# PEER neuron table on one core: 32 of the 384 dense tokens move to the gathered side, and the gathers are placed anew

## The reference, cut to what matters

```python
q = (t @ w_query).reshape(T, PEER_HEADS, 2, PEER_HALF)
s = jnp.einsum('thpk,pnk->thpn', q, sub_keys)
s_val, s_idx = lax.top_k(s, PEER_TOPK)                 # 16 of 128 keys, twice per head
cand = s_val[..., 0, :, None] + s_val[..., 1, None, :]
best, pos = lax.top_k(cand.reshape(...), PEER_TOPK)    # 16 experts per head
expert = ...                                           # 8 heads x 16 = 128 experts per token
gate = jax.nn.softmax(best, -1)
act = gelu(einsum('td,ted->te', t, u_emb[expert])) * gate
out = einsum('te,ted->td', act, v_emb[expert])
```

## Time and profile before

| | |
|---|---|
| median of the three runs | 3464.65 us |
| the profiled execution | 3466.85 us |
| its span | 3465.0 us, 1.85 us lie around it |
| granted TensorE clock, mean | 0.992 |
| TensorE matmul busy | 98% of the span |
| VectorE, ScalarE, GpSimd busy | 62%, 34%, 53% |
| moved by DMA | 874.71 MB, 252 GB/s over the span |

### The profile page before, as it was taken

The page is one execution under the profiler, slowest core; times in us unless marked ns, Lnnn a source line. Parts: engine busy times, 40 slices in busy tenths (PEclk is TensorE's granted clock), DMA queues, the critical chain, the costliest instruction groups (busy, mean ns, idle before and its releaser), DMA issues.

```text
span 3465.0 us, 44031 instructions
## 1 busy us (share of the span) xinstructions
PE 3378.7 (98%) x16931; PEld 2932.8 (85%) x16931; DVE 2155.6 (62%) x3280; ACT 1186.4 (34%) x1632; POOL 1829.8 (53%) x904
## 2 busy tenths in 40 slices
PE   6999999999999999999999999999999999999998
PEld 3688888766888899999999999998887888888887
DVE  2288887746414759993766676644655566556656
ACT  3322221234223232223555556533232232222223
POOL 1210000213444355676666666666877777777775
PEclk8999999999999999999999999999999999999999
DMA  9655643565423236776677777788888878878872
GB/s 380 245 191 202 217 163 115 176 229 204 172 97 146 86 141 234 265 295 267 265 302 300 311 270 284 313 314 332 339 309 317 335 290 342 332 281 313 340 278 108
DMA packets 184618, 874.71 MB, mean 252 GB/s; under 512 B 16621, under 2 KB 77501, under 8 KB 97844
## 3 DMA queue, kind: packets, MB, share of 16 engines
q1 hardware_dynamic: 122160, 525.38, 41.1%
q0 software_dynamic: 38688, 281.15, 20.4%
q10 hardware_dynamic: 23652, 66.69, 5.1%
HBM read 803.78 MB, written 69.32 MB: 252 GB/s over the span
## 4 chain that ended last, share of the span: by engine, by line
PE 85%; DVE 7%; DMA 3%; POOL 2%; issue 1%; ACT 1%; ACTq 0%; SPq 0%; DVEq 0%; POOLq 0%
PE bank L2120 80%; PE bank L2381 2%; DMA ring<-in_w_mod 2%; PE bank L2498 1%; POOL split L807 1%; DMA ring<-in_v_emb 1%; PE bank L2355 1%; DVE b L1880 1%; POOL low L765 1%; DVE rows_a L1819 1%; PE bank L2128 1%; DVE b L1860 0%; DVE rows_c L1819 0%; PE bank L2481 0%; DVE tiny L1875 0%
## 5 line engine op out<-in xcount | busy, mean ns | idle before, releaser
L807 POOL TENSOR_TENSOR split<-ring,split 128x1024 fp32r<-128x1024 f32 x544 | 1343.2, 2481 | 569.4 <-ACT split L1145 567.2
L2120 PE MATMUL bank<-h_hi,split 128*128 128x384 f32 (+1 forms) x4608 | 1221.8, 341 | 8.2 <-POOL split L807 6.9
L2120 PE MATMUL bank<-split,a_split 128*128 128x512 f32 x4608 | 1051.4, 390 | 15.2 <-POOL split L807 15.0
L1145 ACT ACTIVATE split<-ring 128x1024 fp32r<-128x1024 f32 x544 | 574.0, 1060 | 1437.2 <-PE bank L2120 1257.9
L2120 PEld LDWEIGHTS bank<-split,a_split 128*128 128x128 f32 x4608 | 864.5, 188 | 201.8 <-POOL split L807 18.5
L2120 PEld LDWEIGHTS bank<-h_hi,split 128*128 128x128 f32 x4608 | 839.7, 188 | 29.6 <-POOL split L807 8.8
L2120 PE MATMUL bank<-h_lo,split 128*128 128x384 f32 (+1 forms) x2304 | 785.6, 341 | 0.0
L2120 PEld LDWEIGHTS bank<-h_lo,split 128*128 128x128 f32 x2304 | 433.5, 188 | 9.5
L1995 DVE TENSOR_TENSOR acc<-acc,bank 128x512 f32<-128x512 f32 x180 | 121.9, 682 | 331.0 <-PE bank L2120 331.0
L2120 PE MATMUL bank<-hT_hi,w_hi 128*128 128x512 f32 (+1 forms) x768 | 289.3, 377 | 5.3 <-POOL ring_lo L727 2.2
L2120 PE MATMUL bank<-hT_lo,w_hi 128*128 128x512 f32 (+1 forms) x768 | 287.2, 374 | 0.0
(11 more groups left out here) (318 smaller groups left out, 3846.0 us busy)
## 6 DMA issues: line engine op xcount, KB each, us to landing
ring<-in_u_emb SPq DMA_DIRECT2D x128, 1024.0 KB, 4.8
ring<-in_v_emb SPq DMA_DIRECT2D x128, 1024.0 KB, 10.4
ring<-in_w_mod SPq DMA_DIRECT2D x48, 1024.0 KB, 8.2
ring<-in_w_in SPq DMA_DIRECT2D x44, 1024.0 KB, 5.9
ring<-in_w_mod SPq DMA_DIRECT2D x64, 512.0 KB, 4.7
neurons<-tiny ACTq DMA_DIRECT2D x128, 192.0 KB
gate_table<-b ACTq DMA_DIRECT2D x6, 4096.0 KB, 15.0
weigh<-neurons SPq DMA_DIRECT2D x32, 768.0 KB
```

Source lines behind the costliest of these rows:

```text
L807: nc.gpsimd.tensor_tensor(split[:, r % 2, 1, at].bitcast(F32R), ring[:, r % 4, :, :].rearrange("p k n -> p (k n)")[:, at], split[:, r % 2, ...
L1145: nc.scalar.activation(split[:, q % 2, 0, at].bitcast(F32R), ring[:, q, :, :].rearrange("p k n -> p (k n)")[:, at], ACT.Copy)\
L2120: last = mm(out_, left[a].bitcast(F32R), right[b].bitcast(F32R), start=start and n == 0, stop=stop and n == 2)
```

## The change

The last 32 tokens of the third dense tile (EXTRA = 32) are taken out of the neuron matmuls, which have TN = 352 columns instead of 384. Their 32 x 128 slots are spread over four groups of partitions: partition 32g + t holds slot 32g + m of token t in gather m, so that 32 more gathers of `u_emb` and 32 more of `v_emb`, each of 128 rows, carry them. One more plain DMA brings the 32 tokens' rows, copied four times over the partitions, in place of the last tile's rows before their dots; ScalarE copies it into `bank_rows` (neuron unit 119). The v sums of the four groups are copied to SBUF, and four matmuls with a selection matrix (`sel`, not rounded) add them over the groups into the last tile's banks in sweep units 41, 43, 45 and 47. The search, the table and the sweep's matmuls still take all 384 tokens; the neurons of the 32 are zero.

`h2_hi` and `h2_lo` are laid out in blocks of 32 tokens, where it was 128, in the query projection too. ScalarE's and TensorE's loops over the sweep are unrolled in part. The order of the gathers comes from a list: `ROW_UNIT[n]` is the unit in which VectorE uses n. Worked out for the 321 rows (0 to 127 are the u rows of the last tile, 128 the plain one, 129 to 160 the 32 u rows more, 161 to 192 the 32 v rows, 193 to 320 the 128 v rows):

- one a unit in units 3 to 115, two in units 48, 56, ... 112, two a unit in 116 to 125, four in 126;
- in the sweep, two a unit in units 0 to 6 and one in unit 8: the last of the dots;
- v rows from sweep unit 11 to unit 116, at most two a unit, none where k = 7: 160 in 93 units (it was 128 from unit 3 to 115);
- a u row is gathered behind r = 16 + unit - 1, as before, a v row behind r = 16 + unit (with unit counted on from 128), one unit later in relation to its use than before.

```diff
+EXTRA = 32
+EG = P // EXTRA
+TN = TD - EXTRA
+U_ROWS = SLOTS + 1 + EXTRA
+ALL_ROWS = U_ROWS + EXTRA + SLOTS
...
+def row_units():
+
+    at = list(range(3, 3 + PRE - 3))
+    for unit in range(PRE, NK - 2):
+        twice = unit >= PRE + CHUNKS * CHUNK_UNITS or (EXTRA > 16 and unit % 8 == 0)
+        at += [unit] * (2 if twice else 1)
+    at = at[:U_ROWS - 4] + [NK - 2] * 4 if len(at) > U_ROWS - 4 else at + [NK - 2] * 4
+    unit = NK
+    while len(at) < U_ROWS:
+        if unit % 8 != 7:
+            at += [unit] * min(2, U_ROWS - len(at))
+        unit += 1
...
-            h2_hi = region("h2_hi", 8192, search)[:, :].rearrange("p (j k t) -> p k j t", j=LT, t=P)
+            h2_hi = region("h2_hi", 8192, search)[:, :].rearrange("p (g k t) -> p k g t", k=KT, t=EXTRA)
...
+                if n == SLOTS:
+                    pool.wait_ge(e_moved, 16 * 3 * EG)
                 if n >= 3:
                     pool.wait_ge(rows_used, n - 2)
...
+                if n == SLOTS:
+                    pool.dma_start(gathered_rows[n % 3], extra_dram[:, :]).then_inc(gathered[n % 3], 16)
+                    return
...
-                if 0 <= r - (U0 + 2) < SLOTS:
-                    gather_rows(r - (U0 + 2))
-                for m in range(SLOTS):
-                    if V0 + 2 + m - m // 8 == r:
-                        gather_rows(SLOTS + m)
+                for n in range(ALL_ROWS):
+                    if U0 + ROW_UNIT[n] - (n < U_ROWS) == r:
+                        gather_rows(n)
...
+                if r == 4:
+                    act.wait_ge(h2_made, 2)
+                    for g in range(EG):
+                        act.dma_start(extra_dram[g * EXTRA:(g + 1) * EXTRA, :], sh2_row[extra, :]).then_inc(e_moved, 16)
...
-                nc.scalar.activation(neuron_out[:, q % 2, :], bank[:, 4 + q % 2, 0:TD], ACT.Gelu)\
+                nc.scalar.activation(neuron_out[:, q % 2, 0:TN], bank[:, 4 + q % 2, 0:TN], ACT.Gelu)\
...
+                if k == ROW_UNIT[SLOTS]:
+                    rows = gathered_rows[SLOTS % 3]
+                    act.wait_ge(gathered[SLOTS % 3], 16 * (SLOTS // 3 + 1))
+                    act.wait_ge(rows_used, SLOTS)
+                    nc.scalar.activation(bank_rows[:, 0:D - P], rows[:, 0:D - P], ACT.Copy)
+                    nc.scalar.activation(h2_last, rows[:, D - P:D], ACT.Copy).then_inc(rows_used, 1)
...
+                if unit == E_COPY:
+                    act.wait_ge(rows_used, U_ROWS + EXTRA)
+                    nc.scalar.activation(sum_e, bank_rows, ACT.Copy).then_inc(e_copied, 1)
...
+                if k == 8:
+                    nc.vector.scalar_tensor_tensor(sc2_row[wide, :], x2[wide, JD - 1, :], rstd2[wide, JD - 1:JD],
+                                                   sc2_row[wide, :], ALU.mult, ALU.mult).then_inc(a2_made, 1)
...
             weigh_group(0)
-            dot(NK - 5)
+            dot(ROW_UNIT.index(NK - 2))
+            dot(ROW_UNIT.index(NK - 2) + 1)
             rest_group(0)
             weigh_group(1)
-            dot(NK - 4)
             rest_group(1)
+            dot(ROW_UNIT.index(NK - 2) + 2)
+            dot(ROW_UNIT.index(NK - 2) + 3)
...
-                while k < 7 and rows_added < SLOTS and 3 + rows_added - rows_added // 8 <= unit:
-                    add_rows(rows_added)
-                    rows_added += 1
+                for n in range(U_ROWS, ALL_ROWS):
+                    if ROW_UNIT[n] == NK + unit:
+                        add_rows(n)
...
                     for k in range(h * 8, h * 8 + 8):
-                        last = mm3(bank[:, 4 + q % 2, 0:TD].rearrange("p (j t) -> p j t", t=P),
+                        last = mm3(bank[:, 4 + q % 2, 0:TN].rearrange("p (g t) -> p g t", t=EXTRA),
                                    [split[:, q % 2, w, k * P:(k + 1) * P] for w in range(2)],
-                                   [h2_hi[:, k, 0:JD, :], h2_lo[:, k, 0:JD, :]], k == 0, k == KT - 1)
+                                   [h2_hi[:, k, 0:TN // EXTRA, :], h2_lo[:, k, 0:TN // EXTRA, :]], k == 0, k == KT - 1)
...
+                    if extra_rows and s and j == JD - 1:
+                        at = k // 2 * NB
+                        mm(bank[:, 4 + o % 4, :], sel, sum_e[:, at:at + NB], start=False, stop=False)
```

138 lines of the change are left out of this document (105 added, 33 removed).

## The result

The changed kernel takes **3581.93 us** (median, 3576.33 to 3584.39) where the kernel before took 3465.29 beside it (3460.77 to 3469.7): the ratio is 1.0327, 95% interval 1.0304 to 1.035. It is 117 us slower; the forecast was 32 us faster, with a range up to 3480. The profiled execution's span is 3582.0 us, its mean granted clock 0.979 (0.992 before).

A forecast was written before the change was run, and what follows sets the result against it. TensorE was taken as the bound, with VectorE in the search and GpSimd's queue, then DMA, in the sweep close behind. Terms -68 + 3 + 14 + 14 + 6 = -31 us gave 3433 us, range 3392 to 3480.

The forecast's parts named there:

- neuron matmuls, search: Neuron phase: 352 columns save 0.64 us a unit, 8 us up to unit 34 and 60 behind it; -68 us.
- reads in blocks, query projection: Operand reads in blocks of 32 words: counted as nothing, up to 1 ns a matmul (6 us) kept for the range.
- table and turn, up to the sweep: Table's 72 units +3 us for extra dots; turn from neurons to sweep +14 for gathers that come late.
- steady sweep, its beginning: Sweep: +26 us for late v loads, -12 for present waits taken away; +14, bounds -12 and +65.
- small parts: `sel` matmuls +3 us, row swap and a 2048-word copy +2, query projection operations and `extra_dram` wait +1; +6.
- rival (d): Neuron matmuls and query projection: slower reads in blocks of 32 words take back the gain; 3465 to 3500 us, chance 0.03.
- Rival (c): Neuron phase: weight loads set the pace, so fewer columns bring nothing; +37 us, 3502, chance 0.02.
- The wait behind dot 28: End of search: gather 31 waits for VectorE's dot 28, so unit 34 starts at 1549.1 at the earliest, 8 us gained.
- it fits on the mean: Steady sweep: eight units move 24.2 MB at 363 GB/s, DMA share 0.93, below the windows' 410 GB/s.
- rival (b): Sweep: gathers waiting for adds in GpSimd's queue delay splits and TensorE; +96 us over 13 turns, 3527 in all, chance 0.20.
- -12 for the later gathers: Sweep: gathering v rows one unit later removes the second gather's 6.88 us wait at k = 0; -12 us.
- The forecast's check: Signs of error: neuron phase gains under 55 us, or sweep longer by over 45 or shorter; split waits of 100 mean GpSimd's queue.

The follow-up runs named there:

- exp. 3: Kernel before with 352 columns in blocks of 32 words, none of the new gathers: 3435.77 us, ratio 0.9915.
- exp. 1: Kernel before with h2_hi and h2_lo laid out and read in blocks of 32 words instead of 128, still 384 columns: 3491.17 us, ratio 1.0081.
- experiments 11: Kernel before with neuron matmuls of 288 columns, three blocks of 96 words: matmuls 133.3 ns apart, one execution 3336.29 us.
- 12: Kernel before with neuron matmuls of 256 columns, two blocks of 128 words: matmuls 120.0 ns apart, one execution 3336.01 us.
- Experiments 9: Changed kernel with the gathers of u rows from the 105th on half as wide: 3570.9 us.
- experiment 10: Changed kernel with the dots from the 33rd on lacking their second, 128-word part: 3561.17 us.
- 13: Changed kernel with u gathers from the 105th on half as wide and dots from the 33rd on without their 128-word part: 3550.49 us, ratio 1.0257.
- experiment 14: Changed kernel with pairs of u gathers spread over units 44 to 125, v gathers from sweep unit 6, row swap in unit 106: 3548.89 us, ratio 1.0244.
- experiment 8: Changed kernel with 16 tokens moved instead of 32, 368 columns in blocks of 16 words: 3500.78 us, ratio 1.0107.

## Why the prediction was wrong

The sum had five terms. Table and turn are one row here, and the second row is a cost that the sum had at nothing (us):

| term | predicted | measured | from |
|---|---|---|---|
| neuron matmuls, search | -68 | -40 | exp. 3: -31.4, less 8.7 of the query projection |
| reads in blocks, query projection | 0 | +8.7 | exp. 1: 768 x 11.3 ns |
| table and turn, up to the sweep | +17 | +49 | 1341.1 - 1291.9 (changed, exp. 3) |
| steady sweep, its beginning | +14 | +92 | 1159.2 - 1067.3 |
| small parts | +6 | within the above | |

The rows add up to 110. The rest of the 117 us are 6.2 at the start, which are not the change's, and 1.0 by which the sweep of experiment 3 is longer than that of the kernel before.

**Neuron matmuls.** "At the 2.4 GHz level 32 columns are 13.3 ns" was right (experiments 11 and 12). "No row shows such a read, I take nothing and keep up to 1 ns a matmul, 6 us" was the first step that failed: it is 4.4 ns a matmul, and 11.3 in the query projection, which the text named in rival (d) alone. So a unit gives 0.43 us and not 0.64, and the 94 units behind the search give 40 us and not 60: in experiment 3 it is 789.3 us from unit 34 to the sweep, before 829.0. Rival (d) was right in its mechanism; experiment 1, the blocks without the fewer columns, ended at 3491. Rival (c), weight loads, is out: 120 ns with the same load.

**The search.** The wait behind dot 28 does hold unit 34, as forecast. The 8 us that the sum counted as gained up to there did not come. "VectorE does 30 dots in the search, and the change leaves it its work" failed here: the work is the same, but VectorE needs 8.1 us more for it, beside splits that now come in pairs. Unit 34 started 22 us later than the forecast 1549: 6.2 from the start, 8.7 from the query projection, and these 8. It is as late without the gathers (1566.9 in experiment 3, whose start is 4.6 us earlier). That a faster TensorE, which frees `split` earlier, makes the splits pair up is the likely reason; it was not tried by itself.

**Table and turn.** +3 and +14 with bounds of 15 and 28. The table's stage lost 13.5 us, 9.5 more than in experiment 3, in its bounds. The turn was over its bound: some 40 us before the sweep alone. The step that failed is "A cycle of one buffer is 7.45 us and a dot of 2.4, so three buffers give one row in 3.3 us". The dots in the turn's chain were 5.0 to 6.2 us where splits ran beside their second part, and the landings in it 8.6 to 18.4. The prediction took both durations from rows in which one gather a unit ran, and VectorE was costed by its busy time. Experiments 9, 10 and 13 show that the two add 24 us over the whole way to the sweep, and experiment 14 that the turn's idle time goes when its gathers stand further apart. How the rest of the turn divides is open: the landing of 18.4 us beside the last table store (4 MB, 19.4 us from 2280.0), the lower clock, and the row swap, for which VectorE waited 11.3 us where "block the gathered side for some 3 us each" was forecast.

**The sweep.** This is the larger part. That "it fits on the mean", 363 GB/s against windows of 410, was true and no argument. A mean below the peak says nothing about how long one gather takes to land, nor about how soon the next one must follow. The step that failed is "For this I take 2 us in each of 13 turns of eight, +26", which prices late loads and no late gathers. The prediction had the mechanism in rival (b), "from about 12 us on, which DMA near its limit may give, each pair of gathers takes TensorE with it". That (b)'s 96 us are near the measured 92 is luck: it took 52 places at 1.85 us, and the kernel's plan has 74 units with two gathers in the sweep, 1.2 for each. With all its terms (b) ends at 3527, 55 us short. Landings in its chain of waits from 2700 to 2900 are 10.7, 10.9, 11.3, 7.3, 13.7 and 9.0 us. The chain picks the late ones; the medians are 9.4 to 9.9 with whole rows (experiments 9, 10, 13) and 7.2 to 8.8 with half the bytes on either side, where TensorE lacks 20 and 27 us in place of 78.5. Experiment 8 lands its rows in 9.5 to 9.9 as well and lacks 17, with pairs in 51 units. So late landings alone do not cost it, nor pairs alone; both together do. Rival (b) had a chance of 0.20. Missing was also that it would not stay alone: matmuls behind stalls run at the lower clock (31 us more of matmul time in the sweep), and VectorE runs `weigh` and `a_split` beside runs of splits (33 us of TensorE's idle time).

The Trainium skill, "DMA: Bandwidth & Descriptors", section Specifications, gives 358 GB/s as a core's share. The trace still disagrees with it as a ceiling (395 in the window above). The forecast needed 363 on the mean, and the steady sweep got 330. The figure would not have priced the loss either: both experiment 8 and the changed kernel stay under it, at 334 and 330, and only one of them stalls much.

**-12 for the later gathers** was the right mechanism, and too small: alone it is worth 16.4 us of the sweep, 19.6 of the medians. How much of it is left in the changed kernel, where GpSimd waits behind other pairs (2.30 us at 2753.74), no run shows.

**The forecast's check** named what would show it wrong: the neuron phase under 55 us of gain, the sweep longer by over 45, 100 us of splits waited for. The first two came. The third did not: the waits for splits are 44 us, inside the 15 to 50 that stood for the forecast itself, and beside them come 33 us of `a_split` and the lower clock, which no sign named. Nor did the share of DMA rise to 0.9 to 0.95 in the sweep; it is 0.84.

## What to carry to other kernels

Work that is moved from the bound engine to a half idle one is to be priced by the queues there: how long a transfer takes to land when the queues are fuller, how soon the next one must follow, and who stands behind it, not whether the bytes fit on the mean. Where two streams share the DMA engines, a run with either of them halved shows cheaply whether the latency comes from their sum. And look first at the waits that the stream has already: one line that shifts its gathers by a unit gained 20 us, two thirds of what the fewer columns would have brought without their gathers.

## What the runs showed of the hardware that was not expected

**The moving operand's blocks.** Distance of matmuls, each with its own weight load: 512 columns in blocks of 128, 32 and 16 words 226.8, 238 and 242 ns; 384 in blocks of 128 and 32 words 173.3 and 178; 354 in 118 words 163.5 (160.8 by columns); 352 in 32 words 164.4 (160.0); 368 in 16 words 174.4 (166.7); 288 in 96 words 133.3 (133.3).

**VectorE held by a run of GpSimd's instructions.** In the rows read here an operation with both inputs in SBUF that meets GpSimd's splits lasts until the whole run of them is over, one, two or four: 3.17 us beside one and 5.49 beside two for the same operation of the search, 4.13 beside two for one that takes 0.28 alone, 9.35 beside four for one of 1.75. The dots' first part, with one operand in PSUM, keeps its 2.15 us. The Trainium skill, "SBUF — State Buffer", section Who interferes with whom, has it that such an operation contends with a GpSimd instruction that reads SBUF, and that what they contend for is an exclusive lock. The traces agree, and add that the block lasted over four instructions (9.35 us beside 9.47), not one. Taking the second parts away (experiment 10) freed VectorE, which was busy 243.1 us in place of 275.6 from 1540 to 1900.

**A stall costs more than itself.** A unit's 48 matmuls took 10.14 us behind a stall and 7.89 else, at a granted clock of 0.78 in the window from 2310.0 to 2320.3.
